# Tile 1's five projections take tile 0's weight buffers and run between the steps of tile 0's attention

## What is computed

```python
h = rms_norm(x, g_mix) * (1 + scale1) + shift1
proj = h @ w_in                       # 1024 x 2496
q_a, lat, k_r, iq, ik, iw, q_b, k_b, v_b, f_b = split(proj)
o_a = dsa_attention(...)              # keys chosen by an index score, top 64
o_b = forgetting_attention(...)       # causal, with a decay per head
x = x + gate1 * (concat(norm(o_a), norm(o_b)) @ w_out)
h2 = rms_norm(x, g_ffn) * (1 + scale2) + shift2
q = h2 @ w_peer_q                     # 8 heads; scores against two key tables
# per token and head the 16 best of 128 x 128 experts, so 128 experts a token
x = x + gate2 * sum(softmax(score) * gelu(h2 . u[expert]) * v[expert])
return rms_norm(x, g_final)
```

## Time and profile before

| | |
|---|---|
| median of 3 runs | 1479.16 us (1478.48 to 1480.18) |
| profiled execution, its own time | 1486.33 us |
| its span | 1484.4 us |
| PE busy | 1354.0 us, 91% of the span |
| DVE busy | 841.1 us, 57% |
| POOL busy | 429.6 us, 29% |
| mean DMA rate | 286 GB/s; 424 to 425 GB/s from 1000 to 1400 us |
| first gather issued | 778.96 us |

### The profile page before, as it was taken

One profiled execution on the slowest core, in us unless ns is written; L12 is line 12 of the kernel. 1 busy time (PEld: TensorE's weight loads), 2 busy tenths in 40 slices (PEclk: granted clock), 3 DMA queues, 4 the chain that ended last, 5 costly groups with the idle time before them and its releaser, 6 DMA issues.

```text
span 1484.4 us, 14879 instructions
## 1 busy us (share of the span) xinstructions
PE 1354.0 (91%) x5314; PEld 872.2 (59%) x5314; DVE 841.1 (57%) x1997; ACT 292.7 (20%) x690; POOL 429.6 (29%) x545
## 2 busy tenths in 40 slices
PE   7999999999999999999988989998989778778776
PEld 6887888898767777667566554444543222222222
DVE  3558451235127667524256567776766767666654
ACT  2023101031010000114423214541221112111101
POOL 0002000120101000000004544564557555655551
PEclk9999999999999999999898998999999999999999
DMA  8343633311557888537339998999999999999995
GB/s 293 115 170 114 227 114 113 120 51 57 171 186 282 309 297 293 204 127 284 113 114 364 423 422 332 395 421 424 424 424 425 425 425 425 425 426 424 425 425 229
DMA packets 119193, 424.52 MB, mean 286 GB/s; under 512 B 10642, under 2 KB 34632, under 8 KB 84176
## 3 DMA queue, kind: packets, MB, share of 16 engines
q0 software_dynamic: 36896, 268.48, 43.7%
q1 hardware_dynamic: 82224, 155.09, 29.0%
HBM read 422.48 MB, written 1.06 MB: 285 GB/s over the span
## 4 chain that ended last, share of the span: by engine, by line
PE 54%; DMA 26%; issue 7%; POOL 7%; ACT 3%; DVE 3%; SPq 0%; POOLq 0%; DVEq 0%; ACTq 0%
PE psum L560 30%; DMA arena<-peer_uv,arena 15%; DMA wr<-peer_uv,arena 7%; PE psum L811 4%; PE psum L1027 3%; POOL wr L2397 3%; POOL arena L2369 2%; DMA xc<-peer_uv,arena 2%; PE psum L787 2%; PE psum L881 1%; PE psum L857 1%; POOL arena L2397 1%; PE psum L608 1%; PE psum L998 1%; PE psum L1045 1%
## 5 line engine op out<-in xcount | busy, mean ns | idle before, releaser
L560 PE MATMUL psum<-hT,wr 128*128 128x256 f32 x1792 | 393.6, 382 | 1.6 <-DVE hT L1583 1.6
L560 PEld LDWEIGHTS psum<-hT,wr 128*128 128x128 f32 x1792 | 342.3, 191 | 51.9 <-issue 5.3
L1027 PE MATMUL psum<-wr,arena 128*128 128x512 f32 x644 | 312.2, 616 | 54.0 <-POOL arena L2369 53.8
L2215 DVE CUSTOM_DVE_ANT_0 wr<-psum,wr 128x1024 f32<-128x1024 f32 x161 | 196.9, 1223 | 148.4 <-DMA wr<-peer_uv,arena 148.3
L1027 PEld LDWEIGHTS psum<-wr,arena 128*128 128x128 f32 x644 | 114.1, 193 | 232.5 <-issue 232.1
L2397 POOL DMA_INDIRECT wr<-peer_uv,arena x161 | 160.8, 999 | 270.0 <-DVE arena L2163 125.4
L1027 PE MATMUL psum<-arena 128*128 128x512 f32 x276 | 135.3, 617 | 27.3 <-POOL arena L2369 27.0
L2369 POOL TENSOR_SCALAR arena<-cst,arena 128x128 f32<-128x128 f32 x256 | 121.8, 476 | 124.7 <-ACT arena L1431 117.1
L1431 ACT ACTIVATE arena<-arena 128x1 f32<-128x1 f32 x256 | 51.0, 202 | 492.8 <-DVE arena L2215 492.3
L1027 PEld LDWEIGHTS psum<-arena 128*128 128x128 f32 x276 | 48.0, 192 | 112.6 <-issue 112.4
L2215 DVE CUSTOM_DVE_ANT_0 arena<-psum,arena 128x1024 f32<-128x1024 f32 x69 | 84.5, 1224 | 50.2 <-DMA arena<-peer_uv,arena 50.1
(11 more groups left out here) (321 smaller groups left out, 1458.7 us busy)
## 6 DMA issues: line engine op xcount, KB each, us to landing
wr<-in_w_in SPq DMA_DIRECT2D x22, 2048.0 KB, 8.4
arena<-in_w_ada SPq DMA_DIRECT2D x12, 2048.0 KB, 9.8
wr<-in_w_up SPq DMA_DIRECT2D x22, 1024.0 KB, 8.0
arena<-piece SPq DMA_DIRECT2D x16, 1024.0 KB, 9.1
wr<-in_w_down SPq DMA_DIRECT2D x5, 2048.0 KB, 9.2
wr<-in_w_a_out SPq DMA_DIRECT2D x2, 2048.0 KB, 8.1
wr<-in_w_b_out SPq DMA_DIRECT2D x2, 2048.0 KB, 8.3
wr<-in_w_o SPq DMA_DIRECT2D x2, 2048.0 KB, 7.7
```

What stands on the lines that cost most here:

```text
L560: mm = nc.tensor.matmul(bank[p % 4][:, f * S:(f + 1) * S], slot(i)[:, k, c:c + P], act[:, k, :], start=k == 0, stop=k == KT - 1)
L1027: mm = nc.tensor.matmul(bank[(6, 0)[t] + half][:, :], diag[:, n % DIAGS, :], gring[slot_of][:, D + half * BANK:D + (half + 1) * BANK], sta ...
L2215: V.tensor_tensor_reduce(gring[slot_of][:, 0:D], h2[t], gring[slot_of][:, 0:D], 1.0, 0.0, ALU.mult, ALU.add, dots[:, t, c:c + 1]).then_inc ...
```

## The change

Tile 1's projections (tok, qb, kb, qa, vb) no longer have pieces of their own. They are done from the blocks of tile 0 while these are in `wr`, on PE between the steps of tile 0's attention and ahead of the first gather. So a block of `w_in_2` is given back after tile 1 has used it, and not after tile 0. The pieces that are left are the 8 of `w_out_2` and `w_peer_q_2`. The queries of branch b get a buffer for each tile (`qbs`), since both are alive at once. Index rows, forget gate and the first two index scores of tile 1 come right behind tile 0's output projection. In the gather loop, tile 1's attention starts at tick 16 and takes a step every 5 sets, instead of at tick 32 and every 4; the later ticks and the set numbers at which slots join are set anew.

```diff
-T_TURN, T_WOUT, T_QUERY = 74, 76, 93
+T_TURN, T_WOUT, T_QUERY = 68, 70, 92
 def att_tick(step):
-    return 32 + 4 * step
+    return 16 + 5 * step
-JOIN = {SLOTS: 1, 82: 3, 116: 2}
+JOIN = {SLOTS: 1, 74: 3, 118: 2}
-    until("qb", w2[:, :, 952:1464], BANK, "pair_ready", PAIR["qb0b"][0] + 1)
+    until("qb", w2[:, :, 952:1464], BANK, "pair_ready", PAIR["qb1b"][0] + 1)
...
-PIECE_FROM = [("w_in_2", 512, 220), ("w_in_2", 732, 220)]
-PIECE_FROM += [("w_in_2", c + h, 256) for c in (952, 1464, 0, 1976) for h in (0, 256)]
-PIECE_FROM += [(w, c, 256) for w in ("w_out_2", "w_peer_q_2") for c in range(0, D, 256)]
+PIECE_FROM = [(w, c, 256) for w in ("w_out_2", "w_peer_q_2") for c in range(0, D, 256)]
...
             index_rows(0)
+            turn("h1a", 1, 0, 6)
+            turn("h1b", 1, 4, 6)
             by_feature(0, "qb", 1)
             for j in range(4):
                 index_scores(0, j)
+            by_token(1, "tok", 0, 440)
             by_feature(0, "kb", 0)
             by_feature(0, "kb", 1)
             logits(0, 0)
             logits(0, 1)
-            by_token(0, "qa", 256)
+            by_feature(1, "qb", 0)
             logits(0, 2)
             turned(0, 0)
+            by_token(0, "qa", 0, 512)
...
             turned(0, 1)
+            by_feature(1, "qb", 1)
             turned(0, 2)
             queries_a(0)
             turned(0, 3)
-            by_token(0, "vb", 256)
+            by_feature(1, "kb", 0)
+            by_token(0, "vb", 0, 512)
...
             turned(0, 4)
+            by_feature(1, "kb", 1)
...
             mixed(0, 4)
+            by_token(1, "qa", 0, 512)
             logits(0, 7)
...
             mixed(0, 6)
+            by_token(1, "vb", 0, 256, "vb1a")
             mixed(0, 7)
-            turn("h1a", 1, 0, 6)
-            turn("h1b", 1, 4, 6)
             turn("mb0", 0, 4, 7)
+            by_token(1, "vb", 256, 256, "vb1b")
...
-            by_token(1, "tok", 220)
+            index_rows(1)
+            forget(1)
+            index_scores(1, 0)
+            index_scores(1, 1)
             turn("g0a", 0, 0, 9)
```

More of the change, by code:

```diff
@@ L849, in turn, with by_token @@
                 mm.then_inc(s["pair_ready"], 1)
-            def by_token(t, name, cols, between=0):
-                o = claim_bank(f"{name}{t}")
-                if t == 0:
-                    weights(at[name])
-                    for k in range(KT):
-                        mm = nc.tensor.matmul(o[:, 0:2 * cols], hT[:, k, tiles_of[t]], slot(at[name])[:, k, :],
-                                              start=k == 0, stop=k == KT - 1)
-                else:
-                    for half in range(2):
-                        if half:
-                            until(between)
-                        w = landed_piece(PIECE[name] + half)
-                        for k in range(KT):
-                            mm = nc.tensor.matmul(o[:, half * cols:(half + 1) * cols], hT[:, k, tiles_of[t]], w[:, k, :],
-                                                  start=k == 0, stop=k == KT - 1)
-                        if half == 0:
-                            mm.then_inc(s["piece_used"], 1)
+            def by_token(t, name, first, cols, claimed=None):
+                o = claim_bank(claimed or f"{name}{t}")
+                weights(at[name])
+                for k in range(KT):
+                    mm = nc.tensor.matmul(o[:, 0:cols], hT[:, k, tiles_of[t]], slot(at[name])[:, k, first:first + cols],
+                                          start=k == 0, stop=k == KT - 1)
                 mm.then_inc(s["pair_ready"], 1)
@@ L873, in by_feature @@
                 o = claim_bank(f"{name}{t}{'ab'[half]}")
-                if t == 0:
-                    weights(at[name])
-                    w = slot(at[name])[:, :, half * 2 * P:(half + 1) * 2 * P]
-                else:
-                    w = landed_piece(PIECE[name] + half)
+                weights(at[name])
+                w = slot(at[name])[:, :, half * 2 * P:(half + 1) * 2 * P]
                 for f in range(2):
@@ L948, in logits @@
                     c = slice(f * n, (f + 1) * n)
-                    mm = nc.tensor.matmul(o[:, c], q[r:r + 64, h // 2, :], k[r:r + 64, h // 2, 0:n], start=True, stop=not br,
+                    q = qb_rows(t, h // 2) if br else qa[:, h // 2, :]
+                    mm = nc.tensor.matmul(o[:, c], q[r:r + 64, :], k[r:r + 64, h // 2, 0:n], start=True, stop=not br,
                                           skip_group_check=True)
@@ L1050, in _ @@
             emptied(pe, "h0b")
-            by_token(0, "tok", 220)
+            by_token(0, "tok", 0, 440)
             forget(0)
@@ L1126, in _ @@
                     nc.tensor.matmul(o[:, 0:P], qpT[r, h, :], keysT[r, :], start=True, stop=True).then_inc(s["pair_ready"], 1)
-            forget(1)
             for j in range(1, 4):
@@ L1374, in copy_q @@
             def copy_q(t, half):
-                copy_bank(f"qb{t}{'ab'[half]}", qb[:, 2 * half:2 * half + 2, :], 2 * P, scale=0.125)
+                copy_bank(f"qb{t}{'ab'[half]}", qbs[t][half], 2 * P, scale=0.125)
             def copy_k(t, half):
@@ L1469, in _ @@
             exps(0, 3)
+            copy_q(1, 1)
             copy_turned(0, 2)
```

130 lines of the change are left out of this document (55 added, 75 removed), and 4 rows, old and new, of the table names.

## The result

The changed kernel takes 1495.29 us in the median of 6 runs (1493.47 to 1496.55). The kernel before, run beside it, takes 1480.6 us (6 runs, 1478.48 to 1486.97). The ratio is 1.0080, with a 95% interval of 1.0066 to 1.0095: slower by 0.8%. I had forecast 1480.8 with a range up to 1489. The profiled execution took 1493.47 us, with a span of 1491.6.

What follows compares the result with a forecast made beforehand. PE was taken to bound the time ahead of the first gather, DMA behind it. Sum A +33.5 and Sum B -31.9 (bytes -19.7, lost time -12.2) gave +1.6 us: 1480.8, range 1474 to 1489.

Steps and rivals of the forecast that it cites:

- Sum A: Ahead of the gathers: the first gather comes +33.5 us later, 35.1 of it moved projections; bounds 28.6 and 41.5.
- The wait for vb's block: Ahead of the first gather: PE waits 3.0 us for vb's block, loadable only after tile 1's second half of qb.
- The clock: Ahead of the gathers: dense projections win back 3.6 of 4.8 us; +0.8 for a pause from output projection to gather.
- Bytes, -19.7: Gather stage: six pieces follow the first gather in place of 14, 8 x 1.049 MB at 425 GB/s.
- the DMA share of 1.01: Behind the first gather: taken to say transfers are the limit, so a microsecond of bytes removed is one gained.
- Lost time at the start, 5.7 to 3.0: First gather to 820: gathers 4 to 6 issued some 5 us sooner, so 3.0 of 5.7 us lost DMA time stay.
- Lost time in tile 1's attention: Windows 880 to 940: projections between sets fill PE; with them gone, 1.0 of 10.5 us lost DMA time stays.
- The windows of 300 to 370 GB/s in tile 1's attention: Sign of being wrong: such windows again, with steps waiting for DVE or POOL's diagonals rather than a transfer.
- 7.3 forecast: Gather stage: lost DMA time left after the change, 3.0 + 1.0 + 3.3, so 12.2 of 19.5 us come back.
- the lost DMA time was not PE's: Tile 1's attention: gathers wait for DVE's dot products, 3 of 12.2 come back; +10.8, 1490; chance 0.35.
- My condition for it, less than 10.8 us back: Gather stage: the slower rival decides once less than 10.8 us of lost time comes back, which is +3.
- The offset I carried over: Whole kernel: runs' median 1479.16, 0.5% below the profiled 1486.33; terms added to it unchanged, giving 1480.8.

Runs made afterwards that it cites:

- the kernel with few bytes: Kernel before, eight late pieces of w_in_2 bringing only 64 of 2048 columns, every instruction in place: 1478.31 us, ratio 0.9972.
- the two pairs with few products: Kernel before, tile 1's projections over 2 of 8 k, pieces whole against 64 columns: 1490.52 and 1475.17 us; with both holds repaired 1480.89 and 1465.10.
- The two repairs of the changed kernel: Changed kernel, second half of tile 1's qb early and its second rotated query ahead of the first logits: 1484.96 us, ratio 1.0029.
- the two repaired kernels: Kernel before with earlier vb copy and second rotated query ahead, 1476.93 us; changed kernel with early second half of qb and that query ahead, 1484.96 us.
- four sets more for DVE: Changed kernel with tile 1's attention four sets later (ticks 20 + 5 per step): 1497.10 us, ratio 1.0098.
- The kernel with the two repairs: Kernel before, ACT's copy of tile 1's vb two gelus sooner and its second rotated query ahead of the first logits: 1476.93 us, ratio 0.9971.

## Why the prediction was wrong

**Sum A, the first gather: right.** Forecast +33.5; found +30.7, or +32.5 from tile 0's first projection, which this execution began 1.8 us sooner. The wait for vb's block was 3.67 (forecast 3.0). The estimate by the Trainium skill, "DMA: Bandwidth & Descriptors", section on the anatomy of one DMA, made that wait shorter, 2.0; here the row decides. The clock came back at the output projection (7.03), and fell at vb (8.65) and at the queries (5.30), as weighed.

**Bytes, -19.7: right as a sum** of what the stage moved, but my reason for it, the DMA share of 1.01, was not enough, as the kernel with few bytes showed. In the change it held because the PE work that stood beside the bytes went too, as the two pairs with few products show (15.3 and 15.8 us for 14.3).

**Lost time at the start, 5.7 to 3.0: right.** From the first gather to 820 are 10.4 us, and the window 800 to 820 moved 20 x 165/425 = 7.8 us of bytes, nearly all of them behind it: 2.6 lost, and from 820 to 840 the rate is 423.

**Lost time in tile 1's attention: the step that failed.** I wrote "I expect 1.0 of 10.5 to stay" and gave as the reason that projections between the sets fill PE. Found: 9.2 stay. In the kernel before the loss began with a wait of 3.54 us on ACT, which my rows did not hold: I read the windows, where PE is full from 900 on, and took the full PE for the cause. It was catching up behind the hold. The changed order took that hold out of the way and uncovered another, pT10 behind lg11. A wait of PE for a bank had no term in my sum. The windows of 300 to 370 GB/s in tile 1's attention, which I had named as a sign of being wrong, are there, with a wait on DVE behind them. The two repairs of the changed kernel bring the loss to 8.8 us in all, against 7.3 forecast. And with the holds out of the kernel before only 13.7 are lost there, so between the two repaired kernels the change wins back 4.9, not 12.2.

By the profiled executions the forecast was +1.6 and +7.2 was found. Lost time came 8.1 us worse (15.4 for 7.3), the first gather 2.8 better, and the tail 0.4 worse.

**The rival "the lost DMA time was not PE's"** came out on its side, 1490 against 1495, but its mechanism, gathers that wait for a busy DVE, did not: four sets more for DVE gave nothing. That its number was the nearest is in part luck. My condition for it, less than 10.8 us back, was met: 4.1 came back.

**The offset I carried over.** I took the sum against 1479.16. With its later runs the kernel before has medians of 1480.6 to 1482.9. The profiled executions differ by +7.2 us, the medians by 14.7, the ratio says +12. Against the median of 1495.29 the forecast missed by 14.5 us: 5.6 are the terms above, and 8.9 this offset. With the lost time as forecast (8.1 less), or with no offset, it would have been within the range up to 1489. Both profiled executions of before (1486.33, 1486.75) lie at the upper end of its runs, and that of the changed kernel at the lower end. Both have their vb projection at 8.5 to 8.6 us and their output projection at 9.6. The kernel with the two repairs has the same list of PE ahead of the gathers, and its timeline reads there:

```profile
716.22 7.03 PE L857 MATMUL psum<-wr,hT 128*128 128x512 f32 x16
...
736.18 8.80 PE L1099 MATMUL psum<-wr,hT 128*128 128x512 f32 x16 [1.23 <-ACT hT L1329]
```

Its first gather comes at 775.88, 3.1 us sooner than that of the earlier trace rows, and in the one with few bytes (7.03 and 7.13) at 774.67. Counted from tile 0's first projection, which these executions began between 670.7 and 672.5, the two are 2.6 to 3.0 us quicker than the two of before. So the clock ahead of the gathers falls or not by the execution, and both profiled ones of before had it low. The changed kernel spreads too: its own list ahead of the gathers reached the first one at 809.62, 809.76 and 812.96 in three executions, and the profiled one was the quickest of its runs. Both together are of the size of the 5 us; but no trace of a quick execution of before, or of a slow one of the changed kernel itself, was caught, so this stays open.

## What to carry to other kernels

When engines run hand-written lists in step with a ring of transfers, look for the wait at which a dent in the rate begins, not for the engine that is full during the dent: an engine that catches up looks just like one that is the bound. An engine ahead of its partner's list gains nothing from less work (here its hold only grew, from 3.54 to 8.73 us); check for each bank, in list order, at which tick its last content is freed. And before bytes are counted as time, see whether another engine is full in the same window: two limits side by side must be relieved together. Relieving both here meant 35 us of PE work ahead of the stage against 19.7 of bytes within it, and with every hold gone that was still a loss of 7 us.

## What had not been expected of the hardware

A hold of PE of 2.65 us cost the windows around it 7.2 us (9.2 lost with it, 2.0 without): the granted clock is 0.50 behind it, a set takes 3.62 us for 1.88, and POOL was without a slot for 8.7 us. Leaving out 22 us of matmuls made the kernel 0.7% slower (ratio 1.0073, 1.0047 to 1.0099), only in part for a reason that a trace shows. With the products of tok thinned, as in those kernels, PE paused ahead of tile 0's expert queries and ran the first of them in 6.64 us for 3.81. And the same list ahead of the gathers reached the first one between 775.88 and 779.28 in four profiled executions.
